# One program per layer for the output projection, the norm, the expert choice and the expert gather, unrolled and tile by tile

## The reference, cut to what matters

```python
        x_lat = x_lat + g1 * y_lat
        h2_lat = modulate(x_lat, p["norm2"], sh2, sc2)
...
def peer(h, p):
...
        q = (hb @ p["peer_wq"]).reshape(PEER_TOKEN_BLOCK, PEER_HEADS, 2, PEER_QDIM // 2)
        s = jnp.einsum("thsd,hskd->thsk", q, p["peer_keys"]).astype(jnp.float32)
        s_top, i_top = lax.top_k(s, PEER_TOPK)
        cand = (s_top[:, :, 0, :, None] + s_top[:, :, 1, None, :]).reshape(
            PEER_TOKEN_BLOCK, PEER_HEADS, PEER_TOPK * PEER_TOPK)
        g_score, c_idx = lax.top_k(cand, PEER_TOPK)
...
        experts = e1 * PEER_KEYS + e2
        gates = jax.nn.softmax(g_score, axis=-1)
        u = jnp.take(p["peer_u"], experts, axis=0)
        act = jax.nn.gelu(jnp.einsum("thkd,td->thk", u, hb).astype(jnp.float32), approximate=False) * gates
        v = jnp.take(p["peer_v"], experts, axis=0)
        return jnp.einsum("thk,thkd->td", act.astype(v.dtype), v)
```

## Time and profile before

| | us |
|---|---|
| median of 3 runs | 4841.05 |
| lowest, highest | 4838.7, 4843.8 |
| the profiled execution | 4838.35 |
| its span in the trace | 4836.5 |

### The profile page before, as it was taken

How to read it: one execution, slowest core, us unless ns; L and a number is a source line. 1 busy time by engine, 2 the same in 40 slices (tenths; PEclk the granted TensorE clock), 3 DMA queues, 4 the chain that set the end, 5 groups by cost and what they waited for, 6 DMA issues and landing times. The chain is left out here.

```text
span 4836.5 us, 42892 instructions
## 1 busy us (share of the span) xinstructions
PE 3941.5 (81%) x11718; PEld 1977.6 (41%) x11718; DVE 3017.2 (62%) x7075; ACT 1093.0 (23%) x2793; POOL 1569.1 (32%) x1383
## 2 busy tenths in 40 slices
PE   7998978688877878878787877799588788778877
PEld 4655744333333333334343433486233333333333
DVE  1514642577777777777777762743477777777776
ACT  2111221122222212222222222353122222222221
POOL 0001300344444444544444430000144444444442
PEclk9998989899999898989898988999799999889989
DMA  4103620799999999999999971001399999999997
GB/s 156 53 19 114 233 96 14 315 418 404 412 405 412 397 414 402 412 403 405 408 408 408 412 313 61 0 1 44 129 417 418 419 409 412 403 402 408 410 402 324
DMA packets 252187, 1462.22 MB, mean 302 GB/s; under 512 B 24672, under 2 KB 64224, under 8 KB 81776
## 3 DMA queue, kind: packets, MB, share of 16 engines
q0 software_dynamic: 184320, 1342.26, 67.6%
q1 hardware_dynamic: 66320, 114.09, 6.9%
q10 hardware_dynamic: 1376, 4.06, 0.2%
HBM read 1458.18 MB, written 2.13 MB: 302 GB/s over the span
## 5 line engine op out<-in xcount | busy, mean ns | idle before, releaser
L1630 PE MATMUL banks<-arena 128*128 128x512 f32 x5120 | 2397.5, 626 | 684.4 <-ACT arena L1665 679.3
L1562 POOL DMA_INDIRECT arena<-experts,arena x1280 | 1496.3, 1169 | 2657.1 <-PE banks L1630 1343.1
L1751 DVE CUSTOM_DVE_ANT_0 arena<-arena 128x1024 f32<-128x1024 f32 x1280 | 1537.4, 1224 | 781.3 <-DMA arena<-experts,arena 682.6
L1630 PEld LDWEIGHTS banks<-arena 128*128 128x128 f32 x5120 | 1013.7, 201 | 2026.0 <-issue 1232.0
L1665 ACT ACTIVATE arena<-arena 128x128 f32<-128x128 f32 x1280 | 407.8, 389 | 446.6 <-DVE arena L1758 422.5
L1658 ACT ACTIVATE arena<-arena 128x4 f32<-128x4 f32 x320 | 66.0, 206 | 1689.3 <-DVE arena L1751 1670.4
L1576 PE MATMUL banks<-arena 128*128 128x512 f32 (+1 forms) x864 | 327.6, 527 | 10.0 <-DMA arena<-wq 10.0
L1576 PEld LDWEIGHTS banks<-arena 128*128 128x128 f32 x864 | 164.7, 192 | 168.6 <-issue 142.8
L484 PE MATMUL banks<-arena 128*128 128x512 f32 (+1 forms) x640 | 208.6, 486 | 1.8 <-PEq L200 1.8
L1011 PE MATMUL banks<-arena 128*128 128x512 f32 x416 | 184.0, 605 | 14.9 <-DMA arena<-l_w_out 8.4
L825 POOL TENSOR_TENSOR arena<-arena 128x256 f32<-128x256 f32 x48 | 30.4, 634 | 507.2 <-ACT arena L722 376.0
(11 more groups left out here) (206 smaller groups left out, 3283.2 us busy)
## 6 DMA issues: line engine op xcount, KB each, us to landing
arena<-l_w_ada SPq DMA_DIRECT2D x48, 1024.0 KB, 5.0
arena<-experts,arena POOLq DMA_INDIRECT x1280
arena<-wq SPq DMA_DIRECT2D x36, 512.0 KB
arena<-l_w_in SPq DMA_DIRECT2D x7, 2048.0 KB, 7.9
arena<-l_w_out SPq DMA_DIRECT2D x4, 1536.0 KB, 12.3
arena<-l_w_o SPq DMA_DIRECT2D x4, 1024.0 KB, 8.5
arena<-gates SPq DMA_DIRECT2D x7, 512.0 KB, 11.8
arena<-l_w_dqkv SPq DMA_DIRECT2D x1, 2688.0 KB, 8.9
```

The source lines that it names most:

```text
L1562: pool.indirect_dma_start(slots[s], None, tbl, bass.IndirectOffsetOnAxis(ap=expert[:, t % 2, k:k + 1], axis=0)).then_inc(land[s]["sem"], 16)
L1630: mm = pe.matmul(core["ps"][:, 2 * (t % 2) + c, :], diag[:, k % (2 * BATCH), :], v[:, D + c * 512:D + (c + 1) * 512], start=(k == 0), stop ...
L1751: dve.tensor_tensor_reduce(u, u, h2[:, t, :], 1.0, 0.0, ALU.mult, ALU.add, dots[:, k:k + 1]).then_inc(dot["sem"], 1)
```

## The change

`out_stage`, `norm_stage`, `mla_down_stage`, `peer_stage` and `store_stage` are gone. One function, `peer_block`, does a layer's output projection, norm, queries, choices and gather in one program without a loop.

- The output weights are loaded in the stage before (`load_out_weights`, in the gate stage and in the attention stage).
- The prologue goes tile by tile: both halves of a tile's projection, and in between the scores of the tile before the last, the turned rows and the queries of the last one. DVE makes the choices of layer 0's first four (layer 1's first two) steps in it.
- The gather goes tile by tile too, all 8 heads of a tile one after the other, and sums them in one pair of PSUM banks; x is read and written once for a tile, 10 times in all where it was 80.
- Choices run ahead of the gather, in a ring of 32. They are made by groups of tiles, (0), (1, 2), (3, 4, 5) in layer 0 and (0), (1, 2, 3) in layer 1, 24 and 16 groups of one head with queries (an "event"); `wq` is so loaded 24 and 16 times (two sides of 0.52 MB each), where it was loaded 9 times a layer, and keys as often. Its layout in HBM is changed so that a partition's part of a load is 4 KB in one piece, where it was eight pieces of 512 bytes. A position is one batch of four gathers. In layer 0 three of four positions carry half a choice, in layer 1 all four do until the choices are all made (44 of 48 and 30 of 32 inside the gather; the last halves at position 116 of 192 and 59 of 128).
- There are 11 slots in layer 0 and 12 in layer 1. ACT copies the scores out of PSUM.
- Layer 0's first 11 gathers wait until the last tile is projected and added. Layer 1's first 8 wait for their choice alone, the next 4 for all projections.
- Layer 1's norm and down projection run inside layer 0's gather for tiles 0 to 4, in 13 positions each from 130, 139, 148, 157 and 168; tile 5 follows the gather. The down weights are loaded after the last query, the up weights once the last slot is free.
- In layer 1 each tile of the output is stored once it is ready.

On PE at the start of layer 0's projection, where the names are: L1011 the output projection, before.

The diff, cut to its core (`signal`, `at` and `up` count a semaphore's value):

```diff
+def load_out_weights(sp, core, weights, base, ow):
+    K = weights.shape[0] // P
+    w = weights.rearrange("(k p) n -> p k n", p=P)
+    for c in range(2):
+        for part, (a, b) in enumerate(((0, K // 2), (K // 2, K))):
+            sp.dma_start(view(core, base + c * K * 512, K, 512)[:, a:b, :], w[:, a:b, c * 512:(c + 1) * 512]
+                         ).then_inc(ow[2 * c + part]["sem"], up(ow[2 * c + part], 16))
+
...
+PEER_MAPS = (
+    {"groups": ((0,), (1, 2), (3, 4, 5)), "halves": 3, "w": RO, "g1": L0 + 15360, "g2": L0 + 17408,
+     "diag": L0 + 19456, "wq": L0 + 20480, "sc": L0 + 22528, "keys": L0 + 24064, "h2": L0 + 3072,
+     "ht": HO, "slots": [RO + n * ROWS for n in range(6)] + [L0] +
+     [L0 + 9216 + n * ROWS for n in range(4)]},
+    {"groups": ((0,), (1, 2, 3)), "halves": 4, "w": RO + SLOT, "g1": HO + 16384, "g2": HO + 17408,
+     "diag": RO, "wq": XO + TL * D, "sc": RO + D, "keys": RO + 2560, "h2": HO + 22528,
+     "ht": HO + 26624, "slots": [HO + n * ROWS for n in range(8)] + [RO + SLOT + n * ROWS for n in range(4)]},
+)
+PREP_AT = (130, 139, 148, 157, 168)
+PREP = 13
...
+    events = [(h, g) for g in groups for h in range(PH)]
+    E = len(events)
+    order = [(h, t) for h, g in events for t in g]
+    index = {ht_: c for c, ht_ in enumerate(order)}
+    first = [index[h, g[0]] for h, g in events]
+    last = [index[h, g[-1]] for h, g in events]
+    event_of = {c: e for e in range(E) for c in range(first[e], last[e] + 1)}
+    EARLY = tiles - 2
+    R = m["halves"]
+
+    def half_at(g):
+
+        n = R * (g // NB) + g % NB
+        if g % NB >= R or n // 2 + EARLY >= steps:
+            return None
+        return n // 2 + EARLY, n % 2
...
+    query_at = {}
+    for e in range(tiles, E):
+        query_at[e] = max(chosen_at[first[e], 0] - 5, query_at.get(e - 1, -2) + 2)
...
+            for i in range(steps):
+                c = index[i % PH, i // PH]
+                pool.wait_ge(rdy["sem"], at(rdy, c + 1))
+                for k in range(TOPK):
+                    u = i * TOPK + k
+                    if u < NS:
+                        pool.wait_ge(omm["sem"], at(omm, 2 * tiles if layer == 0 or u >= 8 else 0))
+                        if layer == 0:
+                            pool.wait_ge(oad["sem"], at(oad, 2 * tiles))
+                    else:
+                        pool.wait_ge(free["sem"], at(free, u - NS + 1))
+                    pool.indirect_dma_start(slots[u % NS], None, tbl,
+                                            bass.IndirectOffsetOnAxis(ap=expert[:, c % RING, k:k + 1], axis=0)
+                                            ).then_inc(land[u % NS]["sem"], up(land[u % NS], 16))
...
+            for t in range(tiles + 2):
+                if t < tiles:
+                    project(t, 0)
+                if t >= 2:
+                    scores(t - 2, 0)
+                    scores(t - 2, 1)
+                if 1 <= t <= tiles:
+                    turn_rows(t - 1)
+                if t < tiles:
+                    project(t, 1)
+                if 1 <= t <= tiles:
+                    query(t - 1, 0)
+                    query(t - 1, 1)
+                    turn_back(t - 1)
+            for g in range(POS):
+                i = g // NB
+                pe.wait_ge(dg["sem"], at(dg, g + 1))
+                if g == 0:
+                    pe.wait_ge(oad["sem"], at(oad, 2 * tiles))
+                elif g % (NB * PH) == 0:
+                    pe.wait_ge(rd["sem"], at(rd, i // PH))
+                for k in range((g % NB) * BATCH, (g % NB + 1) * BATCH):
+                    v = slots[(i * TOPK + k) % NS]
+                    for c in range(2):
+                        mm = pe.matmul(core["ps"][:, c, :], diag[:, k % (2 * BATCH), :],
+                                       v[:, D + c * 512:D + (c + 1) * 512],
+                                       start=(i % PH == 0 and k == 0), stop=(i % PH == PH - 1 and k == TOPK - 1))
+                    mm.then_inc(free["sem"], up(free))
+                if g - 2 in event_at:
+                    scores(event_at[g - 2], 1)
+                if g - 1 in event_at:
+                    scores(event_at[g - 1], 0)
+                    query(event_at[g - 1], 1)
+                if g in event_at:
+                    query(event_at[g], 0)
+                for u, p in preps(g):
+                    prepare(u, p)
+            if layer == 0:
+                for p in range(PREP):
+                    prepare(TT - 1, p)
...
+            for t in range(tiles + 1):
+                if t >= 1:
+                    norm_rows(t - 1)
+                if t < tiles:
+                    gate_out(t, 0)
+                if t >= 1:
+                    high_columns(t - 1)
+                if 2 <= t < tiles:
+                    choose_a(t - 2)
+                    choose_b(t - 2)
+                if t < tiles:
+                    gate_out(t, 1)
+                if t >= 1:
+                    rows_back(t - 1)
+            for g in range(POS):
+                dot_batch(g)
+                if half_at(g):
+                    c, part = half_at(g)
+                    if part == 0:
+                        choose_a(c)
+                    else:
+                        choose_b(c)
+                weigh(g)
+                if g and g % (NB * PH) == 0:
+                    add_tile(g // (NB * PH) - 1)
+                for u, p in preps(g):
+                    prepare(u, p)
+            add_tile(tiles - 1)
+            if layer == 0:
+                for p in range(PREP):
+                    prepare(TT - 1, p)
...
+            stored = 0
+            for e in range(1, E):
+                if layer == 1 and stored < tiles - 1 and query_at.get(e, 0) > NB * PH * (stored + 1) + 4:
+                    store(stored)
+                    stored += 1
+                sp.wait_ge(qmm["sem"], at(qmm, 2 * e - 1))
+                load_side(e, 0)
+                if e >= 2:
+                    sp.wait_ge(smm["sem"], at(smm, 2 * e - 2))
+                    load_keys(e)
+                sp.wait_ge(qmm["sem"], at(qmm, 2 * e))
+                load_side(e, 1)
+            if layer == 1:
...
-            norm_stage(core, 0, 1, TT, view(core, H2_O, TT, D))
-            peer_stage(core, d, 0, TT)
+            peer_block(core, d, 0, col, EVEN_OUT // P)
         if "mix1" in stages:
-            norm_stage(core, 1, 0, TT)
-            mla_down_stage(core, d)
             mla_up_stage(core, d)
             attention_stage(core, d)
+        if "peer1" in stages:
             ot = view(core, OT_O, KD, LAT)
-            out_stage(core, d["l1_w_o"], lambda k, t: ot[:, k, t * P:(t + 1) * P],
-                      lambda c: view(core, RO + (c + 1) * SLOT, KD, 512), KT_O, 1, TL)
-        if "peer1" in stages:
-            norm_stage(core, 1, 1, TL, view(core, H2_O, TT, D))
-            peer_stage(core, d, 1, TL)
-        store_stage(core, d)
-
-
-ALL = ("ada0", "mix0", "peer0", "mix1", "peer1")
+            peer_block(core, d, 1, lambda k, t: ot[:, k, t * P:(t + 1) * P], KD)
+
+
...
-        w = a[f"l{i}_peer_wq"]
-        arrays[f"wq{i}"] = np.concatenate([w, w[:, 0:HW]], 1)
-        keys = a[f"l{i}_peer_keys"].transpose(3, 0, 1, 2).reshape(P, 2 * PH * PK)
-        arrays[f"keys{i}"] = np.concatenate([keys, keys[:, 0:2 * PK]], 1)
+        w = a[f"l{i}_peer_wq"].reshape(KD, P, 2 * PH, SIDE)
+        arrays[f"wq{i}"] = w.transpose(1, 2, 0, 3).reshape(P, 2 * PH * D)
+        arrays[f"keys{i}"] = a[f"l{i}_peer_keys"].transpose(3, 0, 1, 2).reshape(P, 2 * PH * PK)
         arrays[f"experts{i}"] = np.concatenate([a[f"l{i}_peer_u"], a[f"l{i}_peer_v"]], 1)
```

1015 lines of the change are left out of this document (471 added, 544 removed).

## The result

The changed kernel takes 4652.28 us (median; 4648.49 to 4654.25) against 4840.94 for the kernel before; the ratio is 0.9609, 95% interval 0.9592 to 0.9626. The forecast was 4756 with a range of 4660 to 4840. The direction was right, the gain of 188.7 us is more than twice the 84.9 that were forecast, and the time lies 8 us under the range, near the rival R1 (4663).

The account below looks back on a forecast made before the run. Gathers bound by DMA: only bytes and moments with no gather queued count. Terms -46 + 89 - 89 - 44 + 9 - 4 sum to -85, giving 4756 us; range 4660 to 4840 (own range 4690 to 4825).

Parts of the forecast that it names:

- R1: Rival, both gathers: the rings are ample, stops fall to 40 and 27 us, 93 less, total 4663; chance .2.
- A: Front of layer 0: tile-by-tile work bound by PE brings the first gather to 829.5 from 876.49, -46 us (-15 to -55).
- R3: Rival, both layers' fronts: tile-by-tile work is bound by VectorE and ScalarE, 71 us more, total 4827; chance .1.
- B: Layer 0's gather: 54.3 us of loads plus 120 of stops, against 84.9 lost before, +89 us (+9 to +169).
- The slope: In the gather, each us of longer POOL pause or missing queue costs 1.3 us, read from two windows behind choices.
- The slot's life: Layer 0's ring: a slot's 27.4 us from issue to dot equals 11 x 2.49, so one slot fewer costs next to nothing.
- C: Between the layers: one tile's preparation stays in place of six, 39.6 us where 128.5 stood, -89 us (-70 to -95).
- D: Front of layer 1: effective first issue at 79 us against 122.8, -44 us (-20 to -60).
- E: Layer 1's gather: +14 us of bytes, stops 40 against 44.6 left before, +9 us (-4 to +69).
- F: Final store: a quarter of the 2.1 MB, 7.0 us store remains at the end, -4 us (-5 to 0).
- R2: Rival, both gathers: rings run dry at every choice, up to 5.0 and 3.6 us each, total 4924; chance .1.
- R4: Rival, gathers: straight code stalls as the loop does, 16 x 3.5 = 56 us come back, total 4812; chance .1.

Follow-up runs that it names:

- preps_at_end: Changed kernel with the preparations (norm, down projection) of tiles 0 to 4 moved from layer 0's gather to behind it: 4766.9 us.
- even_halves: Changed kernel with the choice cut elsewhere, four instructions and ScalarE's exponential moved from its first half to its second: 4635.1 us, ratio to before 0.9580.
- before_unrolled_noturns: before_unrolled without the semaphore increments nobody waits for, on VectorE and in front of POOL's issues: 4789.4 us.
- after_with_turns: Changed kernel with the seven semaphore increments nobody waits for put back into the first half of a choice: 4672.4 us.
- small_loads: Changed kernel with each load of query weights inside the gathers cut to an eighth: 4603.4 us.
- before_unrolled: Kernel before with its loop over the heads written out on all five engines, nothing else changed: 4796.6 us, ratio 0.9912.

## Why the prediction was wrong, point by point

**A, forecast -46, measured -56.7.** The mechanism stands: PE was the bound, busy in every microsecond at a granted clock of 0.99. Three sizes were off. PE began at 667.90, 2.1 us sooner than the 670. Its own work took 149.4 us, to 817.3, where the terms up to the 5.2 make 154.3 (a query's 32 records took 3.73 us, not 4.2). And "5.2 (last gate and add, and a cold clock at the start)" was 2.5: the clock was not low at the start, PE having turned the gate stage's rows until 666.4. R3 is refuted with it for layer 0, and for layer 1 too, where PE is busy 51.51 of 51.60 us.

**B, forecast +89, measured +25.0: the step that failed.** The bytes were right: 22.81 MB, 54.2 us at 421 GB/s, forecast 54.3; the "some 8" for preparations and changes of tile was, if anything, too much (1.8 for the preparations by preps_at_end). What failed is "at 1.3 per us that makes 0.45 + 3.2 = 3.6 us a choice". From the refilled ring (POOL goes on at 852.72, the twelfth gather's dot follows at 859.41) 756 intervals take 1985.8 us; less 1882.4 and 54.2 that leaves 49 us of stops, where 120 were forecast. The 120 are so 71 too many. Some 6 us are lost again at the start, where the twelfth dot stands 39.6 us behind the first issue and not 33.2 (5.8 and 11 intervals), for which the forecast had no term in layer 0. With the forecast's 8 for the preparations off, some 41 are left for 44 choices and the queries together, under 1 us a choice, where the forecast had 2.2 without the queries. Not all 41 need be the choices': the same account of the kernel before, 84.8 less 20.9 of bytes, 28.6 of returns and 4.4 of short packets, leaves 31 us that a shorter pause didn't touch. Three things were wrong in the 3.6:

- The slope. It came from one pair of windows, 13 and 10 us long. Three runs that change the pause give 0.3 to 0.5 us per us (16.3, 31.8 and -18.1 us for 0.8, 1.4 and -1.2 us at 44 choices: 0.46, 0.52 and 0.34; 6 us of error in a trace are 0.1 to 0.2 of it, and even_halves also lengthens the second half's pause). The first slot taken away gives 0.56 (61 us for 2.49 us of queue) and the second 0.97 (106 us), so the price rises as the ring gets shorter; 1.3 was met nowhere.
- The base. The 0.45 us at 12 slots is no loss that a shorter pause gives back (before_unrolled_noturns).
- The pause itself. It was read from the kernel before, 14.1 us, though the diff takes seven instructions out of the half choice: after, it is 12.4. after_with_turns prices that at 16 of the 64 us.

The slot's life, the second reading that the forecast had beside it ("11 x 2.49 is 27.4 too"), was nearer: no or little loss at 11 slots. It too priced the next slot at almost twice its cost, and only the one after it right. Why 1 us of missing queue costs half a microsecond at 11 slots stays open. Two facts bear on it: 16.2 MB less of loads gave back 29.4 us and not 38.5 (small_loads), and the DMA engines' share is 1.00 from 859.41 on at 411 GB/s, so these stops don't show as idle engines. With 9 slots, where the price is twice as high, the share falls to 0.95.

**C, forecast -89, measured -89.5.** The steps came near, too: the last addition ends 14.5 us after the last dot (12.9 forecast), the norm takes 3.7 (3.7), turning and columns 3.6 (3), the product 12.3 at a granted clock of 0.76 (9.0 and 3 for the clock), the rest 5.0 (8). preps_at_end puts five more preparations there, and 114.0 us come back between the layers.

**D and E, forecast -35, measured -61.0.** D: VectorE's first dot came 88.4 us after layer 1's projection began at 3230.99 (91.5 forecast), POOL went on at 104.3 (109), 29.9 less is 74.4 (79), against 122.8: -48.4 where -44 was forecast. The hole of "some 20 us" is there, but in the queue and not in the dots, which come late and are never more than 6.8 us apart:

```profile
3320.00:3341.00 21.00, 9.78 (x16) 4.24 (x17) 20.59 (x61) 6.04 (x15) 3.29 (x3) 0.67 0.31 106
```

E: from the thirteenth dot (3335.27 + 5.8) to the last 1295.3 us for 499 intervals of 2.49 (1242.5); of the 52.8 left, 14.55 MB take 34.6, as forecast, and the stops are 18 us where 40 were forecast, 0.6 for each choice with its share of the queries. That makes E -12.6, outside its bounds of -4 to +69: its "30 choices at 1.0 (30) and queries 10" was twice too high. before_unrolled corrects the other side: of layer 1's 44.6 us of losses before, the returns were 16.3, not most of it, and the short packets 9.0; the rest, some 19, is what 16 slots left, so 12 slots stop the ring no more than 16 did.

**F, forecast -4, measured -4.1.** From the last dot to the store's issue it is 13.0 us before and 12.9 after; the store of one tile takes 3.0 us (4649.19 to the end) where four took 7.0.

**The rivals.** R1 had .2 and came within 11 us: its words "the stops fall to 40 and 27" against 49 and 18 measured, 67 us in both. That the sums agree is partly luck, since each part is 9 us off, in opposite directions. Of its signs one came (2008.4 us from first to last dot, 2000 said) and one did not: the slices stand at 395 to 415 where "some 415 in all slices" was said. It should still have been the likeliest, since the argument against it was one window at 406 GB/s. R2, the slower side, would have needed 3.3 us a choice; it takes 9 and 10 slots to come to that (under 5 us a choice in layer 0, 1.6 in layer 1), and that kernel, at 4850.6, is only just slower than the one before. R3 and R4 are refuted above.

**The range.** The forecast's "own range 4690 to 4825" doesn't follow from the bounds of B and E: their lower ends together make 4663, their upper ends 4896. Of the terms B, C, D and F lie within their own bounds, A is 1.7 us and E 8.6 us below.
